# The S5 mixer of a fp32 decoder trunk: four tables loaded on ScalarE's queue, state halves turned by ScalarE, a third output buffer

## What is computed

```python
def s5_layer(u, a_re, a_im, b_re, b_im, c_re, c_im, d_skip, log_dt, w_glu):
    ...
    bu = jnp.einsum('blgk,gpk->blgp', ug, B_bar)
    a = jnp.broadcast_to(A_bar, (1, L, G, P))
    ...
    _, states = lax.associative_scan(combine, (a, bu), axis=1)
    y = jnp.einsum('gkp,blgp->blgk', C_mat, states).real.reshape(Bsz, L, Dm)
    y = jax.nn.gelu(y + d_skip.astype(f32) * uf).astype(u.dtype)
    y1, y2 = jnp.split(y @ w_glu, 2, axis=-1)
    return y1 * jax.nn.sigmoid(y2)
```

## Time and profile before

| | us |
|---|---|
| median of 3 runs | 2110.14 |
| lowest, highest | 2110.12, 2112.23 |
| the profiled execution's own time | 2109.24 |
| its span in the profile | 2106.9 |
| mean granted clock of TensorE | 0.992 |

### The profile page before, as it was taken

One profiled execution on the slowest core, in us unless ns is written; L12 is line 12 of the kernel. 1 busy time (PEld: TensorE's weight loads), 2 busy tenths in 40 slices (PEclk: granted clock), 3 DMA queues, 4 the chain that ended last, 5 costly groups with the idle time before them and its releaser, 6 DMA issues.

```text
span 2106.9 us, 26044 instructions
## 1 busy us (share of the span) xinstructions
PE 2045.2 (97%) x10332; PEld 1744.3 (83%) x10332; DVE 1155.7 (55%) x1653; ACT 603.3 (29%) x717; POOL 46.2 (2%) x55
## 2 busy tenths in 40 slices
PE   4999999999999999999999999999998999999998
PEld 3788888998898889888888988888877798888886
DVE  6677556655455436887444566644458564333322
ACT  2322221423323223222222323322231333222222
POOL 2000000000000000000000000000002000000000
PEclk9999999999999999999999999999999999999999
DMA  8455555433233143667544254544766423233221
GB/s 319 144 195 192 187 190 175 141 120 105 75 109 105 65 155 116 200 229 232 183 166 150 94 159 148 169 148 149 243 206 232 158 80 100 100 100 100 90 95 55
DMA packets 246575, 314.90 MB, mean 149 GB/s; under 512 B 31904, under 2 KB 219552, under 8 KB 244128
## 3 DMA queue, kind: packets, MB, share of 16 engines
q1 hardware_dynamic: 214160, 287.32, 41.4%
q10 hardware_dynamic: 32336, 26.48, 3.8%
HBM read 290.44 MB, written 27.53 MB: 151 GB/s over the span
## 4 chain that ended last, share of the span: by engine, by line
PE 76%; issue 15%; DVE 4%; DMA 3%; ACT 1%; POOL 0%; SPq 0%; ACTq 0%; POOLq 0%; DVEq 0%
PE ps L1779 18%; PE ps L1780 18%; PE ps L1781 18%; PE ps L1806 7%; PE ps L1807 7%; PE ps L1810 7%; DMA y_dram<-s_buf 1%; DVE ada_first L972 1%; DMA y_dram<-acc 1%; PE ps L2058 1%; DMA sq<-y_dram 1%; DMA csil<-in_c 0%; DVE w_lo L962 0%; PE ps L1901 0%; PE ps L2049 0%
## 5 line engine op out<-in xcount | busy, mean ns | idle before, releaser
L557 ACT ACTIVATE w_hi<-w_raw 128x1024 fp32r<-128x1024 f32 x352 | 345.9, 1029 | 353.7 <-PE ps L1781 241.1
L962 DVE TENSOR_TENSOR w_lo<-w_raw,w_hi 128x1024 fp32r<-128x1024 f32 x172 | 210.2, 1222 | 371.8 <-ACT w_hi L557 369.9
L1779 PE MATMUL ps<-g_hi,w_lo 128*128 128x512 f32 (+1 forms) x952 | 345.7, 363 | 0.0
L1781 PE MATMUL ps<-g_hi,w_hi 128*128 128x512 f32 (+1 forms) x952 | 344.9, 362 | 0.0
L1780 PE MATMUL ps<-g_lo,w_hi 128*128 128x512 f32 (+1 forms) x952 | 344.9, 362 | 0.0
L1779 PE MATMUL ps<-h_hi,w_lo 128*128 128x512 f32 x880 | 344.2, 391 | 0.3 <-DVE w_lo L962 0.3
L1781 PE MATMUL ps<-h_hi,w_hi 128*128 128x512 f32 x880 | 342.7, 389 | 0.0
L1780 PE MATMUL ps<-h_lo,w_hi 128*128 128x512 f32 x880 | 342.6, 389 | 0.0
L1806 PE MATMUL ps<-h_hi,w_lo 128*128 128x512 f32 x688 | 269.8, 392 | 2.3 <-DVE w_lo L962 2.0
L1807 PE MATMUL ps<-h_hi,w_hi 128*128 128x512 f32 x688 | 268.6, 390 | 0.0
L1810 PE MATMUL ps<-h_lo,w_hi 128*128 128x512 f32 x688 | 212.3, 390 | 0.0
(11 more groups left out here) (264 smaller groups left out, 2314.1 us busy)
## 6 DMA issues: line engine op xcount, KB each, us to landing
w_raw<-in_ffn_w_in SPq DMA_DIRECT2D x86, 1024.0 KB, 6.6
ada_raw<-in_ada_w SPq DMA_DIRECT2D x128, 512.0 KB, 4.6
w_raw<-in_ffn_w_out SPq DMA_DIRECT2D x32, 1024.0 KB, 6.5
w_raw<-in_ret_w_in SPq DMA_DIRECT2D x24, 1024.0 KB, 5.3
w_raw<-in_ffn_w_out SPq DMA_DIRECT2D x16, 768.0 KB, 4.5
tb<-s_rec SPq DMA_DIRECT2D x6, 1536.0 KB, 6.7
w_raw<-in_ret_w_out SPq DMA_DIRECT2D x8, 1024.0 KB, 5.1
w_raw<-in_s_w_glu SPq DMA_DIRECT2D x8, 1024.0 KB, 6.1
```

The costliest lines, as they stand in the source:

```text
L557: copy = lambda o, i: nc.scalar.activation(o, i, ACT.Copy)
L962: V.tensor_tensor(w_lo[k % 2][:, 0:HALF, :], w_raw[k % 2][:, 0:HALF, :], raw_f32(w_hi[k % 2][:, 0:HALF, :]), ALU.subtract).then_inc(w_lo_h ...
L1779: nc.tensor.matmul(o, wl, xh, start=start, stop=False)
L1781: return nc.tensor.matmul(o, wh, xh, start=False, stop=stop)
```

## The change

- **Tables.** Tables 4 to 7 are no longer issued one by one on SyncE's queue. ScalarE issues all eight DMAs behind the Gelu of block 0, once `w_lo_done` says that the first GLU pair has been split, since table 6 now lies in the room of `w_raw`. Table 7 takes that of table 0. The second GLU pair no longer goes through `w_raw`: it is loaded at b = 3 into `w2_raw`, in table 2's room, and its parts go into the rooms of tables 1 and 3. `glu_pair(2)` waits until block 6's outputs are done.
- **Turning.** For both rotations ScalarE copies the halves crosswise (`halves_changed`, two copies of 64 rows), and VectorE multiplies all 128 rows with the sines at once; the signs of the sums change places. The first turn reads PSUM into `tur`, the second `scanned` into the new `tur_out`. VectorE waits for `v_turned` ahead of the scan, and for `scanned_turned` ahead of the second sine product. `decays` has one buffer instead of two and is written a block ahead.
- **Work inside the scan.** Between `scanned` and the second sine product VectorE does `between(b)`: half a weight split in block 0, the other half in block 1, `output_lo(b - 2)` from block 2 on.
- **Third buffer.** `y_in` has three buffers instead of two; SyncE no longer waits for a load of y to land.
- **Filled waits.** `keep_busy` has TensorE do 5 and 6 matmuls whose results nobody reads in the two waits of `us_norm`.

```diff
@@ -120,6 +120,7 @@
...
         h_lo = sb("h_lo", [P, KT, L], F32R)
+        w_raw_at = place["end"]
@@ -178,9 +179,10 @@
...
         tb += [sb(f"tb{2 + k}", [P, REC], F32, g_at + k * HB) for k in range(4)]
-        tables = [*tb, tb[2], tb[3]]
-        w2_hi, w2_lo = ([sb(f"w2_{part}{k}", [P, 8, CW], F32R, h_at + HB * k + 4 * 8 * CW * (part == "lo")) for k in range(2)]
-                        for part in ("hi", "lo"))
+        tables = [*tb, sb("tb6", [P, REC], F32, w_raw_at), tb[0]]
+        w2_raw = [sb(f"w2_raw{k}", [P, 8, CW], F32, g_at + 4 * 8 * CW * k) for k in range(2)]
+        w2_hi, w2_lo = ([sb(f"w2_{part}{k}", [P, 8, CW], F32R, (h_at, g_at)[k] + HB + 4 * 8 * CW * (part == "lo"))
+                         for k in range(2)] for part in ("hi", "lo"))
@@ -198,9 +200,9 @@
...
         zeros_at = right + 4 * D + 2 * 4 * SC * SK
-        decays_at = (g_at + 5 * HB + 4 * L * 3, zeros_at + 4 * NC)
-        decays = [sb(f"decays{r}", [P, L], F32, decays_at[r]) for r in range(2)]
-        assert decays_at[1] + 4 * L <= hop_at
+        decays = sb("decays", [P, L], F32, g_at + 5 * HB + 4 * L * 3)
+        tur_out = sb("tur_out", [P, L], F32, zeros_at + 4 * NC)
+        assert zeros_at + 4 * NC + 4 * L <= hop_at
@@ -232,7 +234,7 @@
...
         gy = [acc[:], s_buf[:, 0]]
-        y_in = [sq[:, 0], sq[:, 1]]
+        y_in = [sq[:, 0], sq[:, 1], s_buf[:, 1]]
@@ -286,7 +288,8 @@
...
         u_out = [sem(f"u_out{r}") for r in range(2)]
-        y_out, yt_in = [sem(f"y_out{r}") for r in range(2)], [sem(f"yt_in{r}") for r in range(2)]
+        y_out, yt_in = [sem(f"y_out{r}") for r in range(2)], [sem(f"yt_in{r}") for r in range(3)]
+        v_turned, scanned_done, scanned_turned = sem("v_turned"), sem("scanned_done"), sem("scanned_turned")
@@ -418,6 +421,8 @@
...
                 def glu_pair(dp):
+                    if dp == 2:
+                        sp.wait_ge(y_done, 7)
@@ -438,17 +443,13 @@
...
                     sp.wait_ge(y_out[b % 2], 16 * (b // 2 + 1))
-                    if b >= 2:
-                        sp.wait_ge(a5_lo, b - 1)
-                    sp.dma_start(y_in[b % 2].rearrange("p (i c) -> p i c", i=SC),
-                                 y_dram[b].rearrange("i p c -> p i c")).then_inc(yt_in[b % 2], 16)
-                    if b + 4 < KT:
-                        sp.wait_ge(yt_in[b % 2], 16 * (b // 2 + 1))
-                        if b >= 2:
-                            sp.wait_ge(y_done, b + 1)
-                        table(b + 4)
-                    if b == 4:
-                        glu_pair(1)
+                    if b >= 3:
+                        sp.wait_ge(a5_lo, b - 2)
+                    sp.dma_start(y_in[b % 3].rearrange("p (i c) -> p i c", i=SC),
+                                 y_dram[b].rearrange("i p c -> p i c")).then_inc(yt_in[b % 3], 16)
+                    if b == 3:
+                        for k in range(2):
+                            sp.dma_start(w2_raw[k][:], glu_w[:, :, CW + (D, 0)[k]:2 * CW + (D, 0)[k]]).then_inc(w_landed[k], 16)
@@ -515,8 +516,7 @@
...
                 pool.wait_ge(xn_done, 4 * KT + 2)
-                for t in decays:
-                    nc.gpsimd.memset(t[:].rearrange("p (g c) -> p g c", c=NC)[:, :, 0:1], 0.0).then_inc(zeroed, 1)
+                nc.gpsimd.memset(decays[:].rearrange("p (g c) -> p g c", c=NC)[:, :, 0:1], 0.0).then_inc(zeroed, 1)
@@ -858,29 +858,47 @@
...
                 def y_hi(b):
-                    act.wait_ge(yt_in[b % 2], 16 * (b // 2 + 1))
-                    copy(gelu_hi[:, b], y_in[b % 2]).then_inc(a5_hi, 1)
+                    act.wait_ge(yt_in[b % 3], 16 * (b // 3 + 1))
+                    copy(gelu_hi[:, b], y_in[b % 3]).then_inc(a5_hi, 1)
...
                     act.wait_ge(w_landed[k], landed(C_GLU + 2 + k, k))
-                    copy(w2_hi[k][:, 0:HALF, :], w_raw[k][:, 0:HALF, :]).then_inc(w_hi_half, 1)
-                    copy(w2_hi[k][:, HALF:8, :], w_raw[k][:, HALF:8, :]).then_inc(w_hi_done, 1)
+                    copy(w2_hi[k][:, 0:HALF, :], w2_raw[k][:, 0:HALF, :]).then_inc(w_hi_half, 1)
+                    copy(w2_hi[k][:, HALF:8, :], w2_raw[k][:, HALF:8, :]).then_inc(w_hi_done, 1)
+                def halves_changed(to, of, done):
+                    for lo, hi in ((slice(0, NS), slice(NS, P)), (slice(NS, P), slice(0, NS))):
+                        copy(to[lo], of[hi]).then_inc(done, 1)
+                def turn_states(b):
+                    act.wait_ge(v_done, b + 1)
+                    halves_changed(tur, ps[:, b % 2], v_turned)
...
                 def decays_of(b):
-                    copy(decays[b % 2][:].rearrange("p (g c) -> p g c", c=NC)[:, :, 1:NC],
+                    copy(decays[:].rearrange("p (g c) -> p g c", c=NC)[:, :, 1:NC],
...
                 decays_of(0)
-                decays_of(1)
+                turn_states(0)
                 for b in range(KT):
-                    if b + 2 < KT:
-                        act.wait_ge(sc_done, b + 1)
-                        decays_of(b + 2)
+                    act.wait_ge(scanned_done, b + 1)
+                    if b:
+                        act.wait_ge(sc_done, b)
+                    halves_changed(tur_out, scanned, scanned_turned)
+                    if b + 1 < KT:
+                        decays_of(b + 1)
+                        turn_states(b + 1)
...
                     A(gy[b % 2], ps[:, 4 + 2 * (b % 2)], ACT.Gelu_apprx_tanh).then_inc(gelu_done, 1)
+                    if b == 0:
+                        act.wait_ge(w_lo_done, C_GLU + 3)
+                        for later in range(4, KT):
+                            act.dma_start(tables[later][:, 0:R_MT], rec[later]).then_inc(tb_in[later], 16)
+                            act.dma_start(tables[later][:, R_MT:REC], lag_rec[later]).then_inc(tb_in[later], 16)
@@ -1147,7 +1165,6 @@
...
                     V.tensor_tensor(v, v, us_shift[:, :, b].unsqueeze(2).broadcast_to(shape), ALU.add).then_inc(us_dve, 1)
-                split_lo_half(C_GLU + 1, 1)
@@ -1667,36 +1684,38 @@
...
-                def scan(b):
+                def scan(b, between):
...
                     dve.wait_ge(v_done, b + 1)
-                    tt(tur[0:NS], v[NS:P], sn[NS:P], M)
-                    tt(tur[NS:P], v[0:NS], sn[0:NS], M)
+                    dve.wait_ge(v_turned, 2 * (b + 1))
                     tt(rot[:], v, ct, M)
+                    tt(tur[:], tur[:], sn, M)
...
                     dve.sem_inc(v_read, 1)
-                    tt(rot[:], rot[:], tur[:], Sb)
+                    tt(rot[:], rot[:], tur[:], A_)
...
                     if b == 0:
-                        dve.wait_ge(zeroed, 5)
-                    st(V.tensor_tensor_scan(scanned[:], decays[s][:], rot[:], 0.0, M, A_))
+                        dve.wait_ge(zeroed, 4)
+                    st(V.tensor_tensor_scan(scanned[:], decays[:], rot[:], 0.0, M, A_))
                     w()
-                    tt(tur[0:NS], scanned[NS:P], sn[NS:P], M)
-                    tt(tur[NS:P], scanned[0:NS], sn[0:NS], M)
+                    dve.sem_inc(scanned_done, 1)
                     tt(rot[:], scanned[:], ct, M)
+                    between()
+                    dve.wait_ge(scanned_turned, 2 * (b + 1))
+                    tt(tur_out[:], tur_out[:], sn, M)
...
                         dve.wait_ge(y_done, b - 1)
-                    tt(v3(s_prev[s][:])[:, :, 1:NC], v3(rot[:])[:, :, 0:NC - 1], v3(tur[:])[:, :, 0:NC - 1], A_)
+                    tt(v3(s_prev[s][:])[:, :, 1:NC], v3(rot[:])[:, :, 0:NC - 1], v3(tur_out[:])[:, :, 0:NC - 1], Sb)
...
                     dve.wait_ge(a5_hi, b + 1)
-                    V.tensor_tensor(gelu_lo[:, b], y_in[b % 2], raw_f32(gelu_hi[:, b]), Sb).then_inc(a5_lo, 1)
+                    V.tensor_tensor(gelu_lo[:, b], y_in[b % 3], raw_f32(gelu_hi[:, b]), Sb).then_inc(a5_lo, 1)
@@ -1707,16 +1726,20 @@
...
+                def between(b):
+                    if b == 0:
+                        split_lo_half(C_GLU + 1, 1)
+                    elif b == 1:
+                        split_lo_rest(C_GLU + 1, 1)
+                    else:
+                        output_lo(b - 2)
                 for b in range(KT):
-                    scan(b)
-                    if b == 0:
-                        split_lo_rest(C_GLU + 1, 1)
-                    if b >= 2:
-                        output_lo(b - 2)
+                    scan(b, lambda: between(b))
...
                     r = slice(part * HALF, (part + 1) * HALF)
-                    V.tensor_tensor(w2_lo[k][:, r, :], w_raw[k][:, r, :], raw_f32(w2_hi[k][:, r, :]),
+                    V.tensor_tensor(w2_lo[k][:, r, :], w2_raw[k][:, r, :], raw_f32(w2_hi[k][:, r, :]),
@@ -1961,14 +1984,21 @@
...
+            def keep_busy(count):
+                for t in range(count):
+                    nc.tensor.matmul(ps[:, 2], w_hi[0][:, t, 0:P], w_hi[0][:, 0:2, :], start=True, stop=True)
             def us_norm(k):
+                pe.wait_ge(w_hi_done, C_GLU + 2)
...
```

(4 more changed lines are left out.)

## The result

| | before | after |
|---|---|---|
| median, us (19 runs each) | 2109.65 | 2115.78 |
| lowest, highest | 2107.47, 2112.23 | 2111.84, 2117.70 |
| profiled execution, span | 2109.24, 2106.9 | 2117.70, 2115.3 |
| mean granted clock | 0.992 | 0.990 |

The change makes the kernel slower: ratio 1.0031 (1.0025 to 1.0037), 6.1 us. The forecast was 2107.5 us, with 2103 to 2111.5 as its range. The profiled execution of after is the longest of its 19, so its trace shows some 2 us more than the median does.

A forecast was written before the change was run, and what follows sets the result against it. TensorE, busy 97%, bounds the kernel, and SyncE's store, load, table loop spaces the blocks. `first_glu(6)` 2.4 us earlier takes 2109.24 to 2106.8; the median's 0.9 gives 2107.7, rounded to 2107.5 us, range 2103 to 2111.5.

The forecast's parts named there:

- Start of the stage: At states(0) in the S5 mixer: fillers keep TensorE's clock full, so states(0) end at 1575.2 instead of 1576.9 us.
- Rival (5): At states(0): the fillers don't keep the clock, 1.7 us more, 2109 us; chance 0.06.
- One scan: VectorE's scan per block: 3.5 us to `scanned`, turn 1.15, then 1.65; 6.3 us instead of 8.0 with output_lo.
- Eight issues: ScalarE behind Gelu of block 0: eight DMA issues take 4.6 us, bounds 4.4 to 9; outputs(1) at 1596.6 us.
- The y trip inside the burst: y(1) stored and loaded during the tables: store 5 us, landing at 1613, TensorE stalls 3.5 us ahead of outputs(3).
- rival (2): y(1)'s store and load held to the burst's end, back by 1615.5: 2.5 us more, 2110 us; chance 0.10.
- The clock behind the stalls: TensorE from outputs(3) on: forecast steps of 8.13 us, with no low-clock term in the sum.
- The way back: From outputs(3): steps of 8.13 us, 3.3 us idle ahead of outputs(7), `first_glu(6)` at 1653.2 against 1655.59.
- rival (3): Ahead of outputs(7): the clock falls in 3.3 us without work, 2.5 us lost, 2110 us; chance 0.13.
- The slower side: Whole kernel slower than 2114.4 us: at most half of rival (4) and a little of unknown waits; chance 0.10.
- ScalarE's issues held by the first tables: Rival (4), ScalarE's queue: issues wait for first tables to land; slower from 10.5 us on; chance 0.09 with unforeseen waits.

The follow-up runs named there:

- the last one: Kernel with later y, one table per block and weight splits moved into ScalarE's waits, without the eleven fillers and their wait on `w_hi_done`: 2103.47 us, 0.9973 against before.

## Why the prediction was wrong

At `first_glu(6)` the trace is 11.4 us behind the forecast (1664.58 against 1653.2). The terms add up to it: 1.6 us by outputs(1), 4.0 from a longer trip of y(1), 1.4 from VectorE's last two operations ahead of outputs(3), and 4.4 from the clock at outputs(3) and (7). The steps, in the prediction's own order:

- **Start of the stage: wrong in this trace.** States(0) were to gain 1.7 us. The clock was at 0.50 from 1568 to 1574, it had fallen before the first filler, so the fillers took 2.48 and 2.91 us instead of 1.1 and 1.4, the small product queued behind them was late, and states(0) started 1.9 us late. Rival (5) priced this at 1.7 us and had 0.06. In the profile of the kernel with moved splits the same fillers kept the clock; there outputs(0) paid.
- **One scan: 1.0 to 1.4 us short.** The turn took 1.21 to 1.28 us (forecast 1.15, bounds 1.0 to 1.3). But the multiply of block 1 took 1.10 and its sum 1.32 us where the earlier trace rows promise 0.69. The second split ended at 1591.1, not 1589.2, 1.0 of it VectorE's. Ahead of outputs(3), turn, multiply and sum took 4.2 us instead of 2.8, for the two slow operations shown above. The prediction had no term for this.
- **Eight issues: right.** From 1591.14 to the next instruction at 1595.41 are 4.27 us, forecast 4.6. Outputs(1) started at 1598.24 instead of 1596.6: 1.0 from the start of the stage, 1.0 from VectorE, less 0.3 at the issues. (After's common event is 1.25 us earlier in the absolute count, which makes 4.4 us late 5.6.)
- **The y trip inside the burst: this is the term that failed.** The store took 7.0 us instead of 5 and the landing at 1613 became 1618.6, so the stall was 5.72 us instead of 3.5. Two things were mis-sized. The burst ended near 1617 instead of 1610: 1.6 us later start, 1.6 of slow start (254 instead of 420 GB/s over the first 4 us; up to 1593 only 6 packets of tables moved, beside 599 short ones of the load of y(0)), and 3.6 of bytes that I left out, since the rows from 1591 to 1617 sum to 9.9 MB, not 8.4 (loads of `moving` and the y trips share them). And I took equal shares from the moment of issue, by the 58 to 58 packets of the earlier trace rows. What happened is rival (2), which I gave 0.10: the store gets its turn late and the load goes after it. (It had the store land at 1609, and 1609.50 was measured, but the store was issued 1.6 us later than forecast, so the match in time is in part luck.) The Trainium skill ("DMA: Bandwidth & Descriptors", Queues, rings and completion order) has an engine change queues only after a packet of several descriptors, by which I had estimated 4 to 7 us for a store's turn. The trace agrees on the first turn: 198 packets of tables, some 12 for each of 16 engines, go from 1602.5 to 1606 without one of SyncE's; the packets behind it go nearly one for one (132 to 134), as in the earlier trace rows, and there the trace differs from the rule.
- **The clock behind the stalls: not in the sum.** I assumed full clock from outputs(2) on. Outputs(3) and most of the states behind them ran at 0.50, and the step from outputs(3) to (4) was 10.8 us instead of 8.13. TensorE by stretch (length, busy, granted clock, DMA share, GB/s), at the first fillers and around outputs(1), (3) and (7), beside the earlier trace rows:

```profile
1568.00:1570.00 2.00, 2.00 (x8) 0.50 0.52 119
1598.00:1601.00 3.00, 2.76 (x13) 0.50 1.09 456
1618.00:1623.40 5.40, 0.01 (x1) 0.88 0.22 52
1623.40:1628.00 4.60, 4.60 (x21) 0.50 0.00 0
1658.30:1663.00 4.70, 4.68 (x22) 0.65 0.16 59
```

- **The way back: right in kind.** The steps of 8.13 us came (1634.20, 1642.33, 1650.46), and so did the gap of 3.3 us ahead of outputs(7), at 3.09. Of 8.9 us to be won back from outputs(3) to `first_glu(6)` only 4.6 came. The clock explains the rest: 2.7 us at outputs(3), and 1.7 at outputs(7) and the first GLU tile, which ran at 0.65. The latter is rival (3), given 0.13.

Above these terms stands a fault of the argument. I looked for the y wait that would hold the turn, found one, and held it for a passing cost of the burst. What the runs show is that the turning cost time in each of the three settings tried: 10.7 us alone, 3.3 in after, and 2.7 with the later y and spread tables. (In all three the two kernels also differ by `between` and the single `decays` buffer.) No rival named that. The slower side held 0.10, and its one mechanism, ScalarE's issues held by the first tables, did not happen.

The traces show one more thing that the turning brought. Between 1576 and 1662 us, each of the eleven profiles with the turning has 9 to 11 operations of VectorE slowed beside one of GpSimd's, 5.4 to 6.8 us in all; the three without it have a single one, a weight split, 1.1 us longer. The slowed ones read two tiles in SBUF. Those that read PSUM took 0.69 us beside GpSimd too, and these are what VectorE does at that moment where it turns for itself. In after this stood on the path with 1.0 us in block 1 and 1.4 ahead of outputs(3). It is read from the traces; no run took GpSimd's work away.

What stays open: why some profiles keep the clock through the fillers and others don't, and how the cost of the turning divides into its place in ScalarE's stream, its semaphores, and these slowed operations.

## What to carry to other kernels

Before handing a piece of a critical loop to a less busy engine, list what stands ahead of it in that engine's order and what each of those waits for: a share of 29% busy says nothing about waits, and a wait that was harmless there now holds the loop. Loosen the slow round trip first (here, ask for y a block later), and only then move loads or work; the same edit, one table per block, cost 6 us before that and won 5 after it. Price a transfer in a burst by all the bytes that run in its time, not by those of the change.

## What the runs showed of the hardware

- Eight loads of 1.5 and 0.5 MB issued in a row on ScalarE's queue hold ScalarE 4.27 us in after, 0.34 to 0.81 each; none waited for an earlier one to land, with 8 MB outstanding.
- A 256 KB load that takes 2.9 us alone takes 9.1 (after) and some 18 us (turning undone in after, issued at 1595.74) beside such a burst on another queue.
- Two copies of 64 rows by 512, crosswise between the halves, cost ScalarE 1.21 us from PSUM and 1.28 from SBUF; two of 128 rows by 504 cost 1.12. Half the rows saved nothing here.
- Ten of VectorE's 0.69 us operations took 1.10 to 1.43 us in after between 1577 and 1633, each beside one of GpSimd's and with both inputs in SBUF. Before has a weight split of 2.34 us instead of 1.22 at 1584.27, beside GpSimd too. In the fourteen profiles all 55 multiplies `rot<-ps,tb` that ran beside GpSimd, with one input in PSUM, took 0.69 us.
- A gap of 3.23 or 3.24 us ahead of outputs(0) was followed by 3.62 us for its sixteen matmuls in after, by 2.60 in the kernel with later y and one table per block, and by 2.00 in the last one. So the same gap cost anything from nothing to 1.6 us.
- In after, a store of y that was issued while ScalarE's queue was busy had its first packet after some 3.6 us and took 7.0 us, a load had its first after 3.3 us. In the kernel with the turning undone a store issued at 1599.19 took 15.2 us.
